# Three down projections: dense blocks against four jobs of seven products

## The reference, cut to what matters

```python
def swiglu(hn, w_gate, w_up, w_down):
    return (jax.nn.silu(hn @ w_gate) * (hn @ w_up)) @ w_down
...
        x = x + (jax.nn.silu(a) * b) @ w_down[l]
```

## Time and profile before

| what | value |
| --- | --- |
| median of 3 runs | 2960.0 us (2959.25 to 2961.18) |
| profiled execution, span | 2958.2 us |
| granted TensorE clock, mean | 0.999 |
| TensorE busy | 2929.2 us, 99% of the span |
| VectorE busy | 1738.2 us, 59% |
| ScalarE busy | 1402.8 us, 47% |
| GpSimd busy | 1201.4 us, 41% |
| first down projection | about 802.2 to 922.1 us |

### The profile page before, as it was taken

One profiled execution on the slowest core, in us unless ns is written; L12 is line 12 of the kernel. 1 busy time (PEld: TensorE's weight loads), 2 busy tenths in 40 slices (PEclk: granted clock), 3 DMA queues, 4 the chain that ended last, 5 costly groups with the idle time before them and its releaser, 6 DMA issues.

```text
span 2958.2 us, 42962 instructions
## 1 busy us (share of the span) xinstructions
PE 2929.2 (99%) x16510; PEld 2457.3 (83%) x16510; DVE 1738.2 (59%) x2589; ACT 1402.8 (47%) x2324; POOL 1201.4 (41%) x846
## 2 busy tenths in 40 slices
PE   8999999999999999999999999999999999999998
PEld 7778888799988877788888898888787888889987
DVE  7974333497823978772116886168777511298832
ACT  6443344455533546664235555244566532355542
POOL 5336575410154543234555214554332354541243
PEclk9999999999999999999999999999999999999999
DMA  5334232233223523223333233344231233333322
GB/s 163 87 114 140 94 129 99 75 115 111 81 100 78 148 72 100 54 72 90 96 96 107 73 117 119 98 102 136 69 97 47 72 97 99 97 97 106 95 97 71
DMA packets 215049, 288.98 MB, mean 98 GB/s; under 512 B 42698, under 2 KB 122626, under 8 KB 213058
## 3 DMA queue, kind: packets, MB, share of 16 engines
q1 hardware_dynamic: 212354, 281.06, 31.6%
q0 software_dynamic: 880, 2.99, 0.3%
q10 hardware_dynamic: 1616, 2.23, 0.2%
HBM read 270.98 MB, written 4.72 MB: 93 GB/s over the span
## 4 chain that ended last, share of the span: by engine, by line
PE 91%; DVE 5%; ACT 2%; issue 1%; DMA 0%; POOL 0%; SPq 0%; ACTq 0%; DVEq 0%
PE half L922 70%; PE half L1251 4%; PE half L1254 4%; PE half L1253 4%; PE half L1410 2%; PE half L1424 2%; PE half L1388 1%; PE half L1393 1%; PE half L1486 0%; DVE arena L2560 0%; PE half L1177 0%; PE half L1194 0%; PE half L1092 0%; DVE arena L3430 0%; DVE rms L2551 0%
## 5 line engine op out<-in xcount | busy, mean ns | idle before, releaser
L3695 POOL TENSOR_TENSOR wL<-slot,wH 128x512 fp32r<-128x512 f32 (+1 forms) x824 | 1175.9, 1436 | 1727.5 <-ACT wH L1610 1725.9
L1610 ACT ACTIVATE wH<-slot 128x512 fp32r<-128x512 f32 (+1 forms) x824 | 506.2, 623 | 930.7 <-PE half L922 922.2
L922 PE MATMUL half<-arena_split,wH 128*128 128x512 f32 (+1 forms) x2432 | 735.9, 385 | 1.0 <-POOL wL L3695 0.6
L922 PE MATMUL half<-nH,wH 128*128 128x512 f32 x1728 | 684.7, 396 | 3.7 <-ACT arena L1623 2.3
L922 PE MATMUL half<-nH,wL 128*128 128x512 f32 x1728 | 673.6, 390 | 0.0
L922 PE MATMUL half<-nL,wH 128*128 128x512 f32 x1728 | 673.2, 390 | 0.0
L922 PEld LDWEIGHTS half<-arena_split,wH 128*128 128x128 f32 x2432 | 451.1, 188 | 93.8 <-POOL wL L3695 2.8
L922 PE MATMUL half<-arena_split,wL 128*128 128x512 f32 (+1 forms) x1216 | 466.4, 384 | 0.0
L922 PEld LDWEIGHTS half<-nH,wH 128*128 128x128 f32 x1728 | 324.4, 188 | 86.1 <-issue 18.5
L922 PEld LDWEIGHTS half<-nH,wL 128*128 128x128 f32 x1728 | 324.4, 188 | 69.2
L922 PEld LDWEIGHTS half<-nL,wH 128*128 128x128 f32 x1728 | 324.7, 188 | 65.5 <-issue 1.4
(11 more groups left out here) (429 smaller groups left out, 4712.9 us busy)
## 6 DMA issues: line engine op xcount, KB each, us to landing
slot<-in_w_in SPq DMA_DIRECT2D x344, 256.0 KB, 2.7
slot<-in_w_down SPq DMA_DIRECT2D x132, 256.0 KB, 2.6
slot<-in_w_up SPq DMA_DIRECT2D x240, 128.0 KB, 2.2
arena<-in_w_up SPq DMA_DIRECT2D x200, 128.0 KB, 2.4
slot<-in_w_branch SPq DMA_DIRECT2D x64, 256.0 KB, 2.6
slot<-in_w_out SPq DMA_DIRECT2D x48, 256.0 KB, 2.6
arena<-arena SPq DMA_DIRECT2D x40, 256.0 KB, 4.4
slot<-in_w_gate SPq DMA_DIRECT2D x48, 128.0 KB, 2.2
```

What stands on the lines that cost most here:

```text
L922: mm = pe.matmul(dst, lhsT, rhs, start=(k == 0 and m == 0), stop=(k == last and m == 2))
L1610: act.activation(wH[:, p, 0:cols], slot[:, s, 0:cols], ACT.Copy).then_inc(weights_high, 1)
L3695: pool.tensor_tensor(wL[:, p, 0:cols], slot[:, s, 0:cols], plainly(wH[:, p, 0:cols]), ALU.subtract)\
```

## The change

In all three down stretches 6 of the 22 feature blocks stay dense, for both output halves. The other 16 make two groups of 8 blocks (1024 features), and each group with each output half is one job of seven products: `ds0` (group 0, half 1), `ds1` (group 0, half 0), `ds2` (group 1, half 0), `ds3` (group 1, half 1). The order on TensorE is `dn0` (6 dense units), `ds0` to `ds3`, `dn1` (6 dense units).

- TensorE: `down_product` waits for the rest of the weights, for the rest of the tokens, and for four of the products (`DOWN_ADDED`) until VectorE has added an earlier product out of the same bank.
- Weights: quarters of a matrix are loaded with 16 transfers of 128 KB a job (`down_quad`), into the area `nout` (which `nH` and `nL` share, so that the first job's loads wait for the last up block) or into `slot`. The products use three buffers in turn, the two halves of `wH`/`wL` and a hole in the hidden blocks.
- GpSimd makes the rests of P1, P6, P2, P7, P3, P4 (1024 elements a partition each), VectorE that of P5.
- VectorE makes 4 sums of weights a job, 4 sums and 7 rests of tokens a group, and 7 additions of 512 elements from PSUM to `hT` a job. Its order is in `down_jobs`.
- ScalarE makes 7 high parts of weights a job and 7 of tokens a group (`down_highs`).
- The squares and early splits of half 0 (`first_state`, the second part of `add_first`) come when the jobs are done, beside the 6 units of `dn1`.
- In the last stretch the 16 transposes follow unit 2 of `bdn1`, ScalarE then copies out the 2048 elements and after that rounds units 4 and 5.
- Some semaphores are merged (`once_turned`, `mem_read`, `group_done` and others) with the same order of work.

```diff
+DENSE = 6
+DOWN_GROUP, DOWN_HALF = (0, 0, 1, 1), (1, 0, 0, 1)
+DOWN_BY_VECTOR, DOWN_BY_GPSIMD = ("P5",), ("P1", "P6", "P2", "P7", "P3", "P4")
+DOWN_TOKENS = {"P1": "B11", "P5": "T1", "P6": "T2", "P2": "B21", "P7": "T3", "P3": "B22", "P4": "T4"}
+DOWN_ADDS = (("P1", 0, 0, 0), ("P5", 1, 1, 1), ("P6", 0, 0, 1), ("P2", 2, 0, 0), ("P7", 0, 1, 1), ("P3", 1, 0, 1), ("P4", 0, 1, 0))
+DOWN_HIGHS = (("B11", "T1", "T2", "B21", "T3", "B22", "T4"), ("B11", "B21", "B22", "T1", "T2", "T3", "T4"))
+DOWN_BANK = {"P1": 0, "P5": 1, "P6": 0, "P2": 2, "P7": 0, "P3": 1, "P4": 0}
+DOWN_ADDED = {"P6": 1, "P7": 3, "P3": 2, "P4": 5}
...
+def down_buffer(j, nth):
+    return (2 - 7 * j - nth) % 3
...
+        def down_weights(j, what):
+            n = down_buffer(j, PRODUCTS.index(what))
+            if n == 2:
+                return ff_high[:, 6:10, half_t:T], ff_high[:, 14:18, half_t:T]
+            return [in_quarters(v[:, 2 * n:2 * n + 2, :]) for v in (wH, wL)]
...
+            def down_quad(name, src, r0, l=0):
+                j = int(name[3])
+                top, left = r0 + P * DENSE + D * DOWN_GROUP[j], T * DOWN_HALF[j]
+                for quad, r, c in (("A11", 0, 0), ("A21", 0, half_t), ("A22", T, half_t), ("A12", T, 0)):
+                    to = in_quarters(down_quads[j % 2][quad])
+                    for k in range(4):
+                        sp.dma_start(to[:, k, :], src[ds(top + r + k * P, P), ds(left + c, half_t)]).then_inc(S[f"down_landed{j % 2}"], 16)
+            def down_last(stage, src, r0, l=0):
+                name, last = f"{stage}dn1", f"{stage}ds3"
+                for u in range(DENSE):
+                    s = ring.slot[(name, u)]
+                    if s // 2 == 3:
+                        down_split(sp, last, "P1", l)
+                        down_summed(sp, last, "S3", l)
+                    elif s // 2 == 0:
+                        down_split(sp, last, "P2", l)
+                        down_summed(sp, last, "S4", l)
+                    else:
+                        down_split(sp, last, ("P7", "P4")[s // 2 - 1], l)
+                    sp.dma_start(slot[:, s, :], src[ds(r0 + u * P, P), ds(T, T)]).then_inc(landed[s], 16)
+            sp.wait_ge(S["once_turned"], 1)
             layer_vecs(0)
-            for g in range(2):
-                load(f"adn{g}", lin(I["w_down"], 0, 512 * g))
...
+            all_split(sp, "adn0")
+            down_quad("ads1", I["w_down"], 0)
+            all_split(sp, "ads0")
+            down_quad("ads2", I["w_down"], 0)
+            all_split(sp, "ads1")
+            down_quad("ads3", I["w_down"], 0)
+            down_last("a", I["w_down"], 0)
             w = I["w_in_2"]
...
+            def down_product(name, what, o, l):
+                j = int(name[3])
+                down_split(pe, name, what, l)
+                pe.wait_ge(S["down_tokens_split"], 7 * down_group(name[0], DOWN_GROUP[j], l) + PRODUCTS.index(what) + 1)
+                if what in DOWN_ADDED:
+                    pe.wait_ge(S["down_added"], 7 * down_job(name[0], j, l) + DOWN_ADDED[what])
+                (wh, wl), (high, rest) = down_weights(j, what), down_tokens(DOWN_GROUP[j], DOWN_TOKENS[what])
+                for f in range(2):
+                    at = DOWN_BANK[what] * T + f * half_t
+                    for k in range(4):
+                        ft = slice(f * P, f * P + P)
+                        pe.matmul(o[:, at:at + half_t], wh[:, k, ft], high[:, k, :], start=(what not in DOWN_ADDED and f == k == 0), stop=False,
+                                  skip_group_check=True)
+                        pe.matmul(o[:, at:at + half_t], wh[:, k, ft], rest[:, k, :], start=False, stop=False, skip_group_check=True)
+                        mm = pe.matmul(o[:, at:at + half_t], wl[:, k, ft], high[:, k, :], start=False, stop=(k == 3),
+                                       skip_group_check=True)
+                mm.then_inc(weights_used, 1)
...
+            def down(stage, l=0):
+                linear(f"{stage}dn0", split(ff_high, ff_rests), l, ready=multiplied(3 * run_of(stage, l)))
+                for j in range(4):
+                    name = f"{stage}ds{j}"
+                    o = fill(name, l)
+                    for what in PRODUCTS:
+                        down_product(name, what, o, l)
+                        if j == 1 and what == "P5" and (stage == "a" or l + 1 < LAYERS):
+                            turn_layer_vecs(run_of(stage, l))
...
-            for k in range(NF - 3):
+            for k in range(DENSE - 3):
                 unit(o, "bdn1", k, split(ff_high, ff_rests), 1)
-                if k == 14:
+                if k == DENSE - 4:
                     fill("bout0", 1)
...
+            def down_high(stage, n, l=0):
+                j, nth = divmod(n, 7)
+                name, what = f"{stage}ds{j}", PRODUCTS[nth]
+                free = ring.product_room[(name, l, nth)]
+                if free > 0:
+                    act.wait_ge(weights_used, free)
+                if what in ("P1", "P2", "P4"):
+                    down_landed(act, name, l)
+                else:
+                    down_summed(act, name, {"P5": "S1", "P6": "S2", "P7": "S3", "P3": "S4"}[what], l)
+                act.activation(down_weights(j, what)[0], down_whole(j, what), ACT.Copy).then_inc(weights_high, 1)
...
+            def down_highs(stage, l=0):
+                def highs(*ns):
+                    for n in ns:
+                        down_high(stage, n, l)
+                done(act, f"{stage}up{NG - 1}", l)
+                highs(0)
+                blocks_high(stage, 0, "B21", l)
+                sums_high(stage, 0, "T3", l)
+                highs(1)
+                blocks_high(stage, 0, "B22", l)
+                sums_high(stage, 0, "T4", l)
+                highs(2, 3, 4)
+                blocks_high(stage, 1, "B11", l)
+                highs(5)
+                blocks_high(stage, 1, "B21", l)
+                highs(6)
+                blocks_high(stage, 1, "B22", l)
+                highs(7, 8, 9)
+                if stage == "a" or l + 1 < LAYERS:
+                    layer_vecs_read(run_of(stage, l))
+                highs(10, 11, 12)
+                product_done(act, f"{stage}ds1", "P6", l)
+                sums_high(stage, 1, "T1", l)
+                sums_high(stage, 1, "T2", l)
+                highs(13, 14, 15)
+                product_done(act, f"{stage}ds1", "P7", l)
+                sums_high(stage, 1, "T3", l)
+                highs(16)
+                sums_high(stage, 1, "T4", l)
...
-            round_units("bdn1", 1, 0, range(SPLITS, 19), 512)
...
-            round_units("bdn1", 1, 0, range(19, NF), 512)
+            round_units("bdn1", 1, 0, range(SPLITS, DENSE), 512)
...
+            def down_weight_sum(stage, j, what, l=0):
+                name = f"{stage}ds{j}"
+                quads = down_quads[j % 2]
+                if what == "S1":
+                    down_landed(dve, name, l)
+                    if j:
+                        down_split(dve, f"{stage}ds{j - 1}", "P3", l)
+                    out, a, b, op = down_sums["S1"], in_quarters(quads["A21"]), in_quarters(quads["A22"]), ALU.add
+                elif what == "S2":
+                    down_landed(dve, name, l)
+                    down_summed(dve, name, "S1", l)
+                    if j:
+                        down_split(dve, f"{stage}ds{j - 1}", "P6", l)
+                    out, a, b, op = down_sums["S2"], down_sums["S1"], in_quarters(quads["A11"]), ALU.subtract
+                elif what == "S3":
+                    out, a, b, op = in_quarters(quads["A21"]), in_quarters(quads["A11"]), in_quarters(quads["A21"]), ALU.subtract
+                else:
+                    down_landed(dve, name, l)
+                    down_summed(dve, name, "S2", l)
+                    down_split(dve, name, "P5", l)
+                    out, a, b, op = down_sums["S4"], in_quarters(quads["A12"]), down_sums["S2"], ALU.subtract
+                dve.tensor_tensor(out, a, b, op).then_inc(S["weights_summed"], 1)
+            def down_rest(stage, j, what, l=0):
+                dve.wait_ge(weights_high, ring.at(ring.before, f"{stage}ds{j}", PRODUCTS.index(what), l, 0) + 1)
+                high, low = down_weights(j, what)
+                rest(low, down_whole(j, what), high).then_inc(S["down_vector_split"], 1)
...
+            def down_add(stage, j, nth, l=0):
+                what, bank, i, t = DOWN_ADDS[nth]
+                before, at = 7 * down_job(stage, j, l), 4 * DOWN_HALF[j] + 2 * i
+                product_done(dve, f"{stage}ds{j}", what, l)
+                same = [n + 1 for n in range(nth) if DOWN_ADDS[n][2:] == (i, t)]
+                if same:
+                    dve.wait_ge(S["down_added"], before + same[-1])
+                to = hT[:, at:at + 2, t * half_t:t * half_t + half_t]
+                dve.tensor_tensor(to, to, in_halves(ps[jobs.half[f"{stage}ds{j}"]][:, bank * T:bank * T + T]), ALU.add)\
```

(77 more changed lines are left out.)

301 lines of the change are left out of this document (206 added, 95 removed).

## The result

The changed kernel takes 3023.1 us (median of 4 runs, 3020.8 to 3025.5) where the kernel before, run beside it, takes 2960.4: a ratio of 1.0211, 95% interval 1.0198 to 1.0223. The forecast was 2998 with a range from 2965 to 3014. It had the direction right, 25 of the 63 us were missing, and the result lies outside its range.

What follows compares the result with a forecast made beforehand. TensorE, busy for 99% of the span, was taken to bound the kernel. Three stretches 11.6 us longer each (34.8, TensorE's saving included) plus 3.7 at the end gave 38.5 us over 2958.2; forecast 2998 us, range 2965 to 3014.

Steps and rivals of the forecast that it cites:

- What TensorE saves: Down stretches: 32 dense units (87.2 us) replaced by 4 jobs (80.8), saving 6.4 us each, 19.3 for three, without waits.
- Prices of the turns: VectorE and GpSimd alternate on SBUF subtractions of 1024 elements: 1.14 us a turn for VectorE, 2.2 for GpSimd.
- The walk: Hand-stepped engine lists over the jobs: a stretch takes 98.8 us against 87.2 dense, 34.8 more for three; chance 0.54.
- the start: Around dn0 and early ds0: loads hide VectorE's taps, VectorE free at about +2, dense addition ends at 4.3 us.
- The tail: Kernel's end: units 4 and 5 rounded after the 1.88 us copy stall TensorE 3.1 and 0.6 us, 3.7 together.
- Rival 3: Down stretches: VectorE waits in full for each of 24 GpSimd rests, 24 us over dense; 3036; 0.07 with all above 3012.
- Rival 1: Down stretches: buffers smooth the turns, only their total counts, 3.3 us a stretch over dense; 2974 us; chance 0.22.
- Rival 2: Jobs: long strided instructions do not hold the shared interface throughout, so TensorE alone bounds them; faster, 2944 us; chance 0.12.

Runs made afterwards that it cites:

- the run with short turns: Changed kernel, but GpSimd makes only one eighth of the elements of 16 of its 24 weight remainders a down stretch; 2976.4 us, ratio 1.0055.

## Why the prediction missed

- **What TensorE saves: the price was right.** Products at full clock take 2.88 us, to the hundredth. That the 19.3 us can be had as time, no run shows.
- **Prices of the turns: right, a little low.** VectorE's 3.4 us beside a remainder is the 1.14 + 2.2 of the forecast. GpSimd's 1024 elements take, with the turn from the start, 2.33 to 2.43 us (forecast 2.40).
- **The step that failed is "The walk", the term of 98.8 us a stretch.** It measured 105.6 on average, 20.4 us over in three, and it is the same 105.6 with TensorE's clock full. Four of its five places were right: stalls came ahead of P6 of job 0, P4 of job 1, P5 and P6 of job 2. The fifth, 2.6 us ahead of P7 of job 0, is not in the changed kernel's trace, where P7 follows P2 without a wait at 18.1 us, behind the slow P6. With the clock full it is there: P2 starts at 13.8 and P7 at 19.4, 2.7 us late. The sizes were too small:
  - the start: the walk had VectorE free at +2 and the dense addition done at 4.3; in the first stretch that addition runs from 822.23 to 824.51, and ends 6.6 us after P1's start. By then GpSimd holds the next turn, S3 takes 3.29, and P6 starts at 10.8 (9.7 in the layers), not 7.9. Job 0 ends at 26.8, 25.7 and 26.6, not 25.0.
  - job 1, in the first stretch: two small waits ahead of P6 and P2 (0.7 and 0.2 us) that the walk did not have; P4 starts at 48.7, not 45.3.
  - from P5 to P6 of job 2 the walk wrote that S3, S4 and T2's rest each wait for a remainder, and gave them 7.9 us. Three pairs of 1.14 + 2.2 are 10.0 by its own prices, and 10.0 were measured in the first two stretches (7.9 in the last, where P5 starts at 57.2). The rule was stated and not applied.
  - each error stays, since VectorE's list is fixed. In the first stretch P5 of job 2 starts at 58.1 (walk 54.4), P6 at 68.1 (62.3), job 3 at 84.8 (77.2), and job 3 takes 22.4 us, not 21.6, with two stalls instead of one.
- **The clock: not foreseen, and not the cause.** Slow products are worth some 7 us a stretch in the profile (89.8 us busy in the first, 82.8 in the run with short turns, whose clock was full there), nearly the 6.8 missing. Without the run that took them away I would have settled on them.
- **The tail: right.** 3.7 us forecast, 3.1 seen as a wait. As time it was 3.4, of which the runs of the two kernels alone would not assure one.
- **Left out:** 1.6 us of wait in dn0 in each of the two layers, since ScalarE rounds T1 and T2 ahead of the first dense units; the walk called the start hidden.
- **Sum:** 20.4 + 3.2 - 0.6 = 23.0 of the 24.6 us between 2998.5 and 3023.1; the remaining 1.6 is within what the runs scatter.
- **The rivals.** Rival 3 (3036) is nearer in its number, not in its mechanism. It has VectorE sit out all 24 remainders. VectorE was busy for 86.6 us with 64 instructions in the first stretch, and for 84.1 with 85 where GpSimd made none: 21 more at 1.14 us are 24, so it waited for some 26 us, twelve turns of 2.2. Still, 0.07 for all above 3012 was too little for a walk with errors of one sign. Rival 1 (2974), in which the order costs nothing, gave a stretch 90.5 us, and 105.6 were measured. Rival 2 fell, and with it the reading of the note in the Trainium skill ("Advanced Engine Details and Errata", Mode Summary) by which only two-port modes let GpSimd and VectorE shut each other out. The note names these modes; it does not say that nothing else does. Here a float32 subtraction of two SBUF tensors went from 1.22 to 3.4 us beside GpSimd, and to 1.6 beside instructions a quarter as long.

No version here beats the dense kernel. Jobs for one of the two groups of blocks alone, which would ask less of VectorE, were not tried.

## What to carry to other kernels

Where VectorE has two inputs in SBUF, GpSimd is no second pair of hands. Here each remainder that GpSimd made cost VectorE 1.1 us of waiting on average (26 us for 24, 13.3 for 12), about the 1.14 us of making it itself, and one wait can be 2.2 us long at the point where TensorE needs the result. So before moving a subtraction to GpSimd, ask what of it lies under VectorE's reads of PSUM or its idle time; only that is gained. A hand-made walk is to be checked against its own prices pair by pair, because on a fixed list its errors have one sign and add up; give the bad side of its range at least one pair a stage. And do not book a slow clock behind waits as a cost before a run without it is faster: fill the waits with useless matmuls and look.

## What the runs showed of the hardware

The granted clock fell to its lower level behind most waits of 1.9 to 5.3 us in a kernel in which TensorE is busy for 97% of the span, and products behind them took 4.0 to 5.3 us; useless matmuls in the waits kept it at 1.00. The length of the wait alone does not decide it: behind the 2.7 us ahead of P4 of job 1 in the last stretch the product took about 3 us. The turn between GpSimd and VectorE was held for one instruction at both lengths tried: S3 beside remainders of 1024 elements took 3.4 us, beside ones of 256 1.6 to 1.75.
